# A two-layer decoder trunk: expert outputs summed in open PSUM banks instead of stored, a sixth weight slot in their place, heads packed in pairs, and a new order of the mixer and of the layer's ends

## The reference

```
h = rms_norm(x); proj = h @ w_in                       # 6688 columns
y_a = (b * conv3(c * u)) @ w_out_a
y_b = attention(q_latent, kv_latent, rotary key) @ w_out_b   # 8 heads, 64 + 32 columns each
y_c = silu(layer_norm(conv31(glu))) @ w_out_c
x += (sum of sigmoid(gate_i) * y_i) @ w_o
h = rms_norm(x)
group = argmax of 4; the best 2 of its 8 experts, weights comb
x += sum over 32 experts of (silu(h @ w_gate) * (h @ w_up) * comb) @ w_down   # 1024 -> 256 -> 1024
x += sigmoid(rms_norm(x) @ w_pg) * (p @ w_ple)
```

## Time and profile before

| | |
|---|---|
| three runs | 1283.62, 1284.39, 1290.13 us |
| the profiled execution | 1284.47 us, of which the span of its instructions is 1282.7 us |
| mean granted TensorE clock | 0.958 of full speed |
| PE busy | 1135.4 us (89%) |
| DVE busy | 566.7 us (44%) |
| ACT busy | 372.2 us (29%) |
| DMA | 300.53 MB, mean 234 GB/s, 418 GB/s while experts stream |

### The profile page before, as it was taken

How to read it: one execution, slowest core, us unless ns; L and a number is a source line. 1 busy time by engine, 2 the same in 40 slices (tenths; PEclk the granted TensorE clock), 3 DMA queues, 4 the chain that set the end, 5 groups by cost and what they waited for, 6 DMA issues and landing times.

```text
span 1282.7 us, 21657 instructions
## 1 busy us (share of the span) xinstructions
PE 1135.4 (89%) x7828; PEld 895.7 (70%) x7828; DVE 566.7 (44%) x1125; ACT 372.2 (29%) x627; POOL 154.6 (12%) x174
## 2 busy tenths in 40 slices
PE   5997879999689998888999978899995999888897
PEld 5985879998565554447989667899984555444596
DVE  3569885345531111114556889654346111111344
ACT  4332333233222221114344124333322222111332
POOL 0112321001000100000102132201000100000001
PEclk9999999999899999999879989999997999999987
DMA  5624963656269999992636269356544999999621
GB/s 163 150 82 121 322 203 91 192 165 178 99 241 418 418 418 416 418 416 73 181 73 176 74 210 313 110 158 177 150 103 179 384 417 418 417 417 418 263 84 65
DMA packets 207324, 300.53 MB, mean 234 GB/s; under 512 B 14064, under 2 KB 172656, under 8 KB 190832
## 3 DMA queue, kind: packets, MB, share of 16 engines
q1 hardware_dynamic: 207216, 299.18, 66.0%
HBM read 298.11 MB, written 1.05 MB: 233 GB/s over the span
## 4 chain that ended last, share of the span: by engine, by line
PE 61%; DVE 13%; SPq 11%; DMA 7%; issue 4%; ACT 2%; POOL 1%; ACTq 0%; DVEq 0%; POOLq 0%
PE ps L664 58%; SPq L538 11%; DMA gu_ring<-in_w_exp_up_dram 7%; DVE work L1588 4%; PE ps L667 3%; DVE wsplit L1493 2%; DVE work L1519 1%; ACT wsplit L1081 1%; DVE ps L1570 0%; DMA work<-in_positions_dram 0%; DVE wsplit L1850 0%; DVE mx L1573 0%; DVE h_pair L1764 0%; ACT work L1081 0%; DVE mx L1572 0%
## 5 line engine op out<-in xcount | busy, mean ns | idle before, releaser
L664 PE MATMUL ps<-h_pair,wsplit 128*128 128x256 f32 x3264 | 426.2, 293 | 21.8 <-ACT wsplit L1081 15.8
L664 PEld LDWEIGHTS ps<-h_pair,wsplit 128*128 128x128 f32 x3264 | 415.1, 200 | 29.5 <-issue 26.4
L1493 DVE TENSOR_TENSOR wsplit<-ring,wsplit 128x1024 fp32r<-128x1024 f32 x136 | 171.0, 1262 | 125.2 <-ACT wsplit L1081 119.5
L1081 ACT ACTIVATE wsplit<-ring 128x1024 fp32r<-128x1024 f32 x136 | 141.2, 1055 | 229.9 <-PE ps L664 141.5
L664 PE MATMUL ps<-gu_ring,hT 128*64 128x256 f32 x1280 | 158.2, 390 | 32.2 <-DMA gu_ring<-in_w_exp_up_dram 22.9
L664 PEld LDWEIGHTS ps<-gu_ring,hT 128*64 128x64 f32 x1280 | 91.4, 139 | 100.3 <-issue 39.7
L664 PE MATMUL ps<-work,ring 128*128 128x256 f32 (+2 forms) x640 | 142.7, 379 | 0.0
L1816 DVE TENSOR_TENSOR pT<-pT,ps 128x128 f32<-128x128 f32 x64 | 18.4, 288 | 269.7 <-ACT pT L1243 269.7
L1081 ACT ACTIVATE work<-ps 128x512 f32 (+5 forms) x124 | 68.4, 555 | 236.7 <-PE ps L667 167.2
L664 PEld LDWEIGHTS ps<-work,ring 128*128 128x128 f32 (+2 forms) x640 | 111.5, 177 | 26.7 <-issue 3.2
L1588 DVE SCALAR_TENSOR_TENSOR work<-work,convT 128x256 f32<-128x256 f32 x240 | 113.9, 542 | 0.2
(11 more groups left out here) (188 smaller groups left out, 954.5 us busy)
## 6 DMA issues: line engine op xcount, KB each, us to landing
ring<-in_w_in_dram SPq DMA_DIRECT2D x104, 512.0 KB, 4.3
gu_ring<-in_w_exp_gate_dram SPq DMA_DIRECT2D x40, 1024.0 KB, 21.6
gu_ring<-in_w_exp_up_dram SPq DMA_DIRECT2D x40, 1024.0 KB, 21.9
down_ring<-in_w_exp_down_dram SPq DMA_DIRECT2D x40, 1024.0 KB, 22.1
lent_down<-in_w_exp_down_dram SPq DMA_DIRECT2D x24, 1024.0 KB, 22.2
ring<-in_w_exp_gate_dram SPq DMA_DIRECT2D x12, 1024.0 KB, 20.2
ring<-in_w_exp_up_dram SPq DMA_DIRECT2D x12, 1024.0 KB, 21.3
lent_gate_up<-in_w_exp_gate_dram SPq DMA_DIRECT2D x12, 1024.0 KB, 21.1
```

What stands on the lines that cost most here:

```text
L664: return nc.tensor.matmul(o, lhsT, rhs, start=first, stop=last)
L1081: return nc.scalar.activation(o, i, ACT.Copy)
L1493: TT(tile_split[:, m, 1, :, :], tile_of(name, m), tile_split[:, m, 0, :, :].bitcast(F32), ALU.subtract).then_inc(tile_low, 1)
```

## The change

It is one diff with four parts.

1. **Experts.** The outputs are no longer stored. ACT copies the down product (64 pairs by 1024, in two halves on 128 partitions) as its high part and DVE takes the low part (`take_high`, `take_low`); DVE builds a selection matrix of the window (`choose`), which says to which token each pair goes; and PE adds the product of both into banks 4 to 7, which stay open over all experts (`combine`, 16 matmuls of 128x256 with 64 rows, upper and lower rows in turn). The pair's weight is multiplied in where the hidden rows are taken (`take_hidden`). Once, at step 1, PE spreads weights, places and window ends over the partitions (`spread`) and writes zeros to the four banks (`clear_sums`). The area of `ys` becomes a sixth weight slot, of which gate and up are loaded after unit `wo1` and down after `spread`.
2. **End of the layer.** Transposes, split and `cb` units go; the sums are added to `x` as they are, the high part of the next input is made straight from `x`, the embedding product starts inside the last expert steps, and `stat("ple")` stands behind `pg0`.
3. **Attention.** Weights of keys and queries are packed by ACT (`pack`) so that two heads fill 128 columns; rotation is one matmul for all heads; even and odd heads have their own zero-padded tiles. 46 taps stand ahead of the first maximum, 5 follow in each of six heads, and 48 stand between the gate units. `ga0` moves into the heads. The branches a and b of all four column blocks come first, then branch c; the layer norm is at the fourth block.
4. **Start of the layer.** The small vectors are loaded ahead of `x`, the first projection stands ahead of `stat("mix")`, the rotary tables cover 128 partitions.

```diff
-ERING = 5
+ERING = 6
-TAPS_BEFORE = [50, 13, 13]
+TAPS_BEFORE = 46
+TAPS_PER_HEAD = 5
+LN_AT = 3
...
+                sp.wait_ge(unit_ready, unit_value(l, "wo1"))
+                sp.sem_inc(wait_carried, 1)
+                load_gate_up(l, OWN + 2, OWN + 2)
...
+                sp.wait_ge(spread_psum, 3)
+                sp.sem_inc(wait_carried, 1)
+                load_down(l, OWN + 2, OWN + 2)
...
+                pe.wait_ge(packed_ready, 1)
-                for i in range(4):
+                for i in range(2):
                     free_bank(f"kn{i}")
                     for j in range(2):
                         for c in range(2):
-                            last = mm(two(bank(f"kn{i}"))[0:NOPE, j, :], ukv[:, c, 2 * i + j, 0:NOPE], kvn[:, c, :], c == 0, c == 1)
+                            last = mm(two(bank(f"kn{i}"))[:, j, :], turned(0, c, 2 * i + j), kvn[:, c, :], c == 0, c == 1)
...
+                def queries():
+
+                    for i in range(3):
+                        free_bank(f"uq{i}")
+                    for i in range(3):
+                        pe.wait_ge(packed_ready, i + 2)
+                        b = (i + 1) % 2
+                        for k in range(2):
+                            c = 2 * i + k
+                            pe.wait_ge(qn_ready, c + 1)
+                            for q in range(2):
+                                mm(bank(f"uq{q}")[:, 0:S], turned_rope(b, k, q), qn[:, c, :], c == 0, c == 5)
+                            for pair in range(4):
+                                o = bank("uq2") if pair == 3 else ps[:, 4 + pair, :]
+                                last = mm(o[:, 0:S], turned(b, k, pair), qn[:, c, :], c == 0, c == 5)
+                        last.then_inc(unit_ready, 1)
...
-                    def turn_out(it, k):
+                    def combine(it, k, final):
                         w = window_of(it, k, per)
-                        pe.wait_ge(yrow_ready, w + 1)
-                        if k >= 2:
-                            pe.wait_ge(ys_ready, w - 1)
-                        pe.sem_inc(wait_carried, 1)
-                        for i in range(4):
-                            last = tr(ps[:, 2 + k % 2, i * P:(i + 1) * P], yrow[:, k % 2, i * P:(i + 1) * P])
-                        last.then_inc(yT_psum, 1)
+                        pe.wait_ge(window_sel_ready, w + 1)
+                        pe.wait_ge(y_low, w + 1)
+                        for part in range(2):
+                            for i in range(4):
+                                for j in range(2):
+                                    rows = slice(j * WIN, (j + 1) * WIN)
+                                    last = mm(two(ps[:, 4 + 2 * j + i // 2, :])[:, i % 2, :], y_part[rows, part, i * P:(i + 1) * P],
+                                              window_sel[rows, k % 2, :], False, final and part == i % 2 == 1)
...
                         if not ending:
                             gate_up(it, k, 0)
+                        if k == 1:
+                            spread()
                         if one_before:
                             turn_hidden(it, k - 1)
+                        if final:
+                            embed(0)
+                        if two_before:
+                            combine(it, k - 2, final)
                         if not ending:
                             gate_up(it, k, 1)
+                        if k == 1:
+                            for b in (4, 5, 6):
+                                clear_sums(b)
                         if one_before:
                             down(it, k - 1)
...
+                project_split("pg0", "ple")
                 stat("ple", [sq_p[:, c, :] for c in range(DC)], sq_events("ple", DC))
-                project_split("pg0", "ple")
-                bcast("ple")
-                for m in range(1, 4):
+                project_split("pg1", between=lambda: bcast("ple"))
+                for m in range(2, 4):
                     project_split(f"pg{m}")
```

More of the change, by code:

```diff
@@ L914, in _ @@
                 last.then_inc(lg_ready, 1)
+                wait_evacuated(pe, "wo2")
+                for i in range(2):
+                    for t in range(TC):
+                        last = tr(bank("wo2")[:, i * S + t * P:i * S + (t + 1) * P], prow[:, t, i * P:(i + 1) * P])
+                last.then_inc(pT_tr, 1)
                 free_bank("rank")
@@ L1125, in _ @@
                 high_rows(hT, [(h_ready, 2 * i + 2) for i in range(4)])
+                act.wait_ge(x_in, 4)
+                squares("mix", sq_x, xT, [None] * 4)
                 high_tiles(l, "q0")
@@ L1145, in _ @@
                     evacuates(copy(v[:, t, :], bank(f"v{t}")), f"v{t}")
[L1147 to L1152 removed]
+                pack(0, "uq1", QK, "kn1")
+                pack(1, "uq2", QK, "uq0")
+                wait_unit(act, l, "uq1")
+                high_tile(l, "c0", 0)
+                wait_unit(act, l, "uq2")
+                high_tile(l, "c0", 1)
+                act.wait_ge(stat_ready, after(NORMS, "q"))
+                for q in range(2):
+                    evacuates(copy(qR[:, q, :], bank(f"uq{q}")[:, 0:S]), f"uq{q}")
+                for pair in range(4):
+                    o = bank("uq2") if pair == 3 else ps[:, 4 + pair, :]
+                    copy(qE[0:NOPE, pair, :], o[0:NOPE, 0:S]).then_inc(q_nope, 1)
+                    last = copy(qO[NOPE:P, pair, :], o[NOPE:P, 0:S]).then_inc(q_nope, 1)
+                act.wait_ge(q_nope, 8)
+                act.sem_inc(evacuated[UI["uq2"] % BANKS], 1)
+                high_tiles(l, FILL[1])
                 def exponentials(h):
@@ L1443, in rstep @@
                 dve.wait_ge(rope_step, n_rope[0])
-            dve.wait_ge(init_loaded, 48)
+            dve.wait_ge(init_loaded, 32)
+            dve.wait_ge(const_set, 1)
+            for r in range(0, P, ROPE):
+                nc.vector.tensor_copy(turn[r:r + ROPE, r:r + ROPE], cst[NOPE:QK, C_ROT + NOPE:C_ROT + QK])
+                last = nc.vector.tensor_copy(turn[r:r + ROPE, P:P + 1], cst[NOPE:QK, C_FREQ:C_FREQ + 1])
+            rstep(last)
+            for r in range(0, P, WIN):
+                last = nc.vector.reduce_sum(row_of[r:r + WIN, :], upper[r:r + WIN, r:r + WIN], AX.X)
+            rstep(last)
+            rstep(TS(row_of[:, :], row_of[:, :], -1.0, float(WIN), ALU.mult, ALU.add))
             a0, a1, a2 = (ang[rows, i, :] for i in (1, 3, 2))
```

666 lines of the change are left out of this document (374 added, 292 removed).

## The result

The changed kernel takes 1245.29 us, the median of four runs (1239.60 to 1248.93); the kernel before took 1284.80 us in the same comparison (1283.62 to 1290.13). The ratio is 0.968, 95% interval 0.963 to 0.973. The forecast was 1270 us in a range of 1212 to 1300. The profiled execution took 1246.42 us with a span of 1244.2, against 1282.7 before: 38.5 us less.

A forecast was written before the change was run, and what follows sets the result against it. Expert stage bound by PE (7.50 us a step) with DMA close; attention by PE and DVE waiting on each other. A layer: +28.1 - 14.3 - 22 + 1 = -7.2; two layers -14.4, from 1284.5 to 1270 us, range 1212 to 1300.

The forecast's parts named there:

- its own test: Forecast wrong if the expert step's period is off by over 0.2 us, or the attention gives under 15 us a layer.
- the attention: Attention stage: fewer PE instructions (11.3 us) and better order, with fewer taps ahead, give 22 us a layer.
- the layer's start: Start of each layer: first projection 4 us earlier but at the lower clock, `x` later; +1 us a layer.
- the ends: End of each layer, last down to last gate unit: 43.7 us instead of 58.0, 14.3 us less.
- the size of combine: Expert step: combine's sixteen matmuls at 0.117 us, 1.87 us, plus 0.10 for changing the array's division; step 7.50 us.
- rival B: Combine's upper and lower rows run beside each other: 0.94 us, step 6.57 us, total 1214 us; chance 22%.
- Steps 2 to 31: Expert stage after step 1: 30 steps of 7.50 us, ending at 608.5 us on the old timeline.
- Step 1: Second expert step: one-time `spread` and `clear_sums` add 6.4 us, so step 2 begins at 383.5, not 377.06.
- the clears: Zeros written to four banks in step 1 by `clear_sums`: 4 x 0.85 us.
- The DMA: Expert weights at 7.54 us an expert: no bound after the change, transfers through at 572 us.
- rival D: Attention gives only its instructions (11 us) as packing, weight loads or DVE's chain hold PE: 1292 us; chance 13%.
- Rival A: The forecast itself: combine bound by its weights, pitches 0.109 to 0.125 us, 1256 to 1288 us; chance 50%.

The follow-up runs named there:

- narrow matmuls: Changed kernel with combine's 16 matmuls streaming only 128 of 256 selection columns, one run with halves in turn, one in sequence: 1242.79 and 1269.98 us.
- half a combine: Changed kernel with combine issuing only the eight matmuls of the high part, low part left out: 1235.66 us, ratio 0.957 to the kernel before.
- five slots: Changed kernel with the sixth slot's lead removed, at most five experts loaded ahead: 1247.93 us, ratio 0.970 to the kernel before.

## Why the forecast was right and wrong

**Right in sign, too small by 24 us** (-14.4 forecast, -38.5 in the profiled executions). By its own test it was wrong: the period was off by 0.78 us where 0.2 was allowed, and the attention gave under 15 us in layer 0. By the table the experts cost 42 us less in both layers than forecast, the attention and the layer's start gave 15 less, and the ends 2.6 less: -42 + 15 + 3 = -24.

**The step that failed: the size of combine.** "I take 0.117 us, 1.87 us for sixteen, and 0.10 for one more change of the array's division." It measured 1.14 us. The cause was right, the weights are the bound (narrow matmuls). The price of one matmul in one half was right as well, some 0.117 us. What failed is that sixteen of them were added up one behind the other. The size came from rows in which each load fills the whole array, and there each waits for the one before it. With halves in turn two loads run beside each other: an added matmul costs 0.059, and the change of division cost 0.2, not 0.10. So rival B's condition held, with 0.059 for its 0.0585; its step of 6.57 lacked only 0.1 us more for the change of division and 0.06 for the transpose of the hidden rows (0.26 for 0.20). The profile before had this: the two column halves of gate and up at 0.113 us a record against the keys' 0.22 in one half were seen and put aside, because the weights there have 64 columns. The Trainium skill, TensorE: Matmul & The Clock Gate, section LDWEIGHTS, gives by its P / 1.2 rule 0.107 us for 128 columns. The first two loads of a half in combine start 0.108 us apart, which agrees; the steady pitch in a half is 0.117. The Trainium skill, TensorEngine Tiling (Array Packing), section Key Properties, says that tiles can load weights and compute in parallel, and with the halves in turn this trace agrees.

**Steps 2 to 31** therefore took 201.7 us and not 225, 23.3 less. Step 1 added 8.9 us and not 6.4. Of the 2.5 us more, 0.9 are `spread` (3.85 for 2.98), 0.9 the gate and up of steps 0 and 1 with the wait between them (11.7 us, before 10.8), 0.4 the clears, and 0.3 the rest of the step. After PE's wait of 4.42 us for the second window the clock is lower (granted at 0.60 from 353 to 361 us), and sixteen records of gate and up take 3.68 us instead of 1.95; but the kernel before had the like (0.66 from 368.3 to 373.3 us), so this is little of the difference. The clears were costed about rightly at 3.4; they measure 3.7 a layer in time.

**The DMA** "through at 572" was right in its kind: the last expert weights are asked for by 546 us and there is no wait, yet with half a combine PE waits in the last seven steps. That the sixth slot counts in case B was wrong: five slots do as well within 3 us. Whether it counts at a shorter step was not tried.

**The attention** gave 13.6 us in layer 0 and 17.6 in layer 1 (111.4 us before, 93.8 now), and not 22. The layer's start, +1 by the forecast, came out at -0.1 and +4.4: in layer 1 the projection begins 3.9 us earlier as foreseen, but the key's product takes 5.14 us for 3.62, one unit 7.48 for 6.00 (granted at 0.79 from 671 to 679 us), and PE waits 1.44 us for the packed weights. The heads' pitch came out better (7.40 for 7.7). What was missed: `u0` was to be done at 125.6 and was at 131.1, since the rotation is counted behind `c0` and the low part of `u0` stands behind two maxima; moving them gave back 5.5 us a layer. The sum went through each engine's own work and left out where in its queue the next tile is made. And `ga0` waited 3.10 us for a chunk behind 3 MB of expert weights, then took 7.49 us for 5.99 (granted at 0.77); this was named under rival D, and its removal shows in the trace and not in the time. The taps' order is worth 5.5 us a layer, less than half of the 12 us of DVE that they take, since DVE had idled for 5 of them.

**The ends** were right: 43.7 forecast, 43.2 measured in layer 0 and 46.2 in layer 1.

**The range.** Rival A's pitches of 0.109 to 0.125 us are 7.7 us either way by its own prices, and not 15. The measured 1245 lies in the whole range only because that reaches down to B's 1214; A alone ended at 1256.

## What to carry to other kernels

Where the array is divided and the weights bound, put neighbours in different halves, and take the price from rows with the array divided, not from full loads. Add up the work of two halves side by side, not in one line. Look for an engine that idles after its releaser is long done: a counter shared by several units holds its reader until all units counted ahead are through. Compare the transfer's time with the step over the whole stage before buying a slot of prefetch: here one more bought nothing, and a shorter step on PE would soon have met the DMA.

## What was not expected of the hardware

- A loop of twelve expert steps with 32 matmuls in combine makes the step of its return 10.3 us longer while 408 GB/s of weights stream (506 to 512 us), and instructions are transferred during the stops. With six steps in the body there is no stall at four returns and no such transfer in the last turns; nor is there with sixteen matmuls and twelve steps.
- Sixteen 64-row matmuls of 128 columns of weights with 256 columns streamed: 1.14 us with the halves in turn, 1.72 in sequence. With 128 columns streamed: 1.04 and 1.54. In one half the starts are about 0.117 us apart in either order; the two halves start theirs 0.003 us apart.
- One matmul that opens a sum in a bank is enough for the sums in the other places of that bank: the four banks needed no zeros, at 7.4 us less.
